# A bidirectional linear recurrence on one core: a table of steps for each compute engine in place of one common order

## What is computed

```python
def wkv_step(S, inp):                      # for each direction and each of 8 heads, S is 64 x 64
    r, w, k, v, a, b = inp
    sa = jnp.einsum('dbhvk,dbhk->dbhv', S, a)
    S = S * w[..., None, :] + sa[..., None] * b[..., None, :] + v[..., None] * k[..., None, :]
    return S, jnp.einsum('dbhvk,dbhk->dbhv', S, r)

S_c, y_c = wkv_bidir(S0, *prep_c[:6])      # context, both directions
_, y_l = wkv_bidir(S_c, *prep_l[:6])       # sequence, from the context's states
rwo_l = rwkv_output(y_l, prep_l, r_k, gn_w, gn_b)
g = jax.nn.sigmoid(gates)                  # gates = h @ w_in[:, ...], 3 x 1024 columns
merged = sum(g[n] * (branches[n] @ w_br[n]) for n in range(3))
```

## Time and profile before

| | us |
|---|---|
| median of three runs | 1972.29 |
| the three runs | 1978.79, 1972.29, 1966.57 |
| span of the profiled execution | 1977.8 |
| TensorE busy in it | 1749.3 (88%) |
| VectorE, ScalarE, POOL busy | 801.0, 518.5, 109.0 |
| mean granted TensorE clock | 0.939 of full speed |

### The profile page before, as it was taken

How to read it: one execution, slowest core, us unless ns; L and a number is a source line. 1 busy time by engine, 2 the same in 40 slices (tenths; PEclk the granted TensorE clock), 3 DMA queues, 4 the chain that set the end, 5 groups by cost and what they waited for, 6 DMA issues and landing times.

```text
span 1977.8 us, 37817 instructions
## 1 busy us (share of the span) xinstructions
PE 1749.3 (88%) x16766; PEld 936.9 (47%) x16766; DVE 801.0 (40%) x1472; ACT 518.5 (26%) x983; POOL 109.0 (6%) x143
## 2 busy tenths in 40 slices
PE   4999999989989999878988999899988987778786
PEld 3444565444546556345555666554543332323332
DVE  3753252646627464345444454325452211122111
ACT  3710252311127322344433431113131110000000
POOL 0000011010000000200000000000000101010100
PEclk8999997989989999989988997899988999998998
DMA  9121475252110200312221221236659999999996
GB/s 392 56 85 43 179 266 205 93 219 97 43 43 1 96 27 0 139 55 62 62 61 50 62 67 35 93 148 235 253 202 356 420 418 420 424 417 422 415 407 201
DMA packets 51560, 359.43 MB, mean 182 GB/s; under 512 B 8392, under 2 KB 8640, under 8 KB 32960
## 3 DMA queue, kind: packets, MB, share of 16 engines
q1 hardware_dynamic: 38896, 311.51, 39.5%
q0 software_dynamic: 12496, 45.45, 7.0%
HBM read 337.99 MB, written 27.32 MB: 185 GB/s over the span
## 4 chain that ended last, share of the span: by engine, by line
PE 69%; DMA 17%; DVE 6%; ACT 5%; issue 2%; POOL 0%; SPq 0%; DVEq 0%; ACTq 0%; POOLq 0%
PE psum L208 66%; DMA arena<-in_w 16%; ACT arena L205 4%; PE psum L211 3%; DVE arena L155 3%; ACT L205 1%; DVE arena L185 1%; DVE arena L165 1%; DVE arena L161 1%; DMA arena<-in_norm_post 1%; DVE arena L193 0%; DMA arena<-in_subln 0%; DVE arena L160 0%; DVE arena L181 0%; DVE arena L173 0%
## 5 line engine op out<-in xcount | busy, mean ns | idle before, releaser
L208 PE MATMUL psum<-arena 32*32 32x16 f32 (+11 forms) x16114 | 1668.5, 309 | 200.0 <-DMA arena<-in_w 82.5
L208 PEld LDWEIGHTS psum<-arena 32*32 32x32 f32 (+5 forms) x16114 | 863.6, 137 | 949.7 <-issue 784.8
L205 ACT ACTIVATE arena<-psum 128x512 f32<-128x512 f32 (+5 forms) x334 | 171.1, 512 | 920.8 <-PE psum L208 714.7
L155 DVE TENSOR_TENSOR arena<-arena,psum 128x512 f32<-128x512 f32 (+3 forms) x128 | 64.9, 507 | 427.7 <-PE psum L208 236.3
L155 DVE TENSOR_TENSOR arena<-arena 128x512 f32<-128x512 f32 (+10 forms) x315 | 191.6, 608 | 47.5 <-DMA arena<-in_norm_post 12.4
L205 ACT ACTIVATE arena<-psum,arena 128x128 f32<-128x128 f32 (+3 forms) x221 | 111.5, 505 | 305.8 <-PE psum L211 154.2
L205 ACT ACTIVATE arena<-arena 128x512 f32<-128x512 f32 (+10 forms) x254 | 138.8, 546 | 195.4 <-DVE arena L155 38.4
L155 DVE TENSOR_TENSOR arena<-psum,arena 128x128 f32<-128x128 f32 (+3 forms) x116 | 47.4, 409 | 194.3 <-PE psum L208 170.5
L211 PE MATMUL psum<-arena 128*128 128x128 f32 x652 | 101.4, 291 | 18.3 <-DMA arena<-fd,arena 8.9
L165 DVE SCALAR_TENSOR_TENSOR arena<-arena 128x512 f32<-128x512 f32 (+7 forms) x158 | 102.1, 646 | 38.2 <-ACT arena L205 33.1
L211 PEld LDWEIGHTS psum<-arena 128*128 128x128 f32 x652 | 75.4, 146 | 80.1 <-issue 52.9
(11 more groups left out here) (49 smaller groups left out, 176.7 us busy)
## 6 DMA issues: line engine op xcount, KB each, us to landing
arena<-in_w SPq DMA_DIRECT2D x127, 2048.0 KB, 25.6
arena<-in_w SPq DMA_DIRECT2D x48, 256.0 KB, 3.0
arena<-in_w SPq DMA_DIRECT2D x10, 1024.0 KB, 26.8
arena<-kd POOLq DMA_DIRECT2D x28, 256.0 KB, 3.8
gd<-arena SPq DMA_DIRECT2D x24, 256.0 KB, 3.2
arena<-gd SPq DMA_DIRECT2D x24, 256.0 KB, 8.4
arena<-in_w POOLq DMA_DIRECT2D x2, 2048.0 KB, 10.0
kd<-arena POOLq DMA_DIRECT2D x2, 1536.0 KB, 9.2
```

What stands on the lines that cost most here:

```text
L155: return self.ends(self.e.tensor_tensor(out, a, b, op))
L205: return self.ends(self.e.activation(out, a, func, **kw))
L208: return self.ends(self.e.matmul(out, lhs, rhs, start=start, stop=stop))
```

## The change

The common order is gone, and with it `WOVEN`, `rec_order` and `gate_steps`. Three tables, written out as text, give each compute engine its own list: `TENSOR_STEPS` (395 entries, 93 of them `gate`), `VECTOR_STEPS` (230) and `SCALAR_STEPS` (130, 24 of them `gate`). `gate` stands for two gate products on TensorE and for the copy of one block on ScalarE. As before, 6 gate products come ahead of the recurrence. Both directions now start together.

Four steps are divided where they wait inside: `kn` into `kn0`, `kn1` and `co` on TensorE; `a` into `gv` and `a` on TensorE; ScalarE's `p1` into `w` and `p1` (one group of four sigmoids each); VectorE's `p2` into `ls` (the scan) and `p2`. The finish's steps `f` have fewer empty places. What each step issues is the same, and each engine has as many instructions as before. POOL gets one more wait.

```diff
-FIRST_GATES = 6
-def gate_steps(order):
...
+FIRST_GATES = 3
+TENSOR_STEPS = """
+p1.00 p1.10 gate gate gate gate gate g1.00 gate g2.00 gate gate gate g1.10 gv.000 x1.00 a.000 kn0.00 g2.10 gate gate gv.100 u1.00 a.100 x1.10 kn0.10
...
+s.151 a.051 gate s.051 m.151 y.15 end.1 m.051 gate y.05 end.0 gate gate gate
+"""
+VECTOR_STEPS = """
+a.000 ls.00 a.100 p2.00 p3.00 ls.10 g1.00 p2.10 p3.10 g2.00 g1.10 x1.00 g2.10 u1.00 x1.10 u1.10 x2.00 x2.10 ls.01 u2.00 x3.00 p2.01 u3.00 p3.01 x4.00
...
+SCALAR_STEPS = """
+w.00 p1.00 gate p2.00 w.10 p1.10 gate p2.10 gate a.000 kn.00 kn.10 w.01 gate p1.01 p2.01 w.11 p1.11 gate a.100 p2.11 gate s.000 a.001 kn.01 s.001 w.02
...
+def steps(text):
+    for s in text.split():
+        name, at = (s.split(".") + [""])[:2]
+        yield (name, *map(int, at), *[0] * (3 - len(at)))
...
@@ gate_tensor
-                    yield
+                    if k % 2:
+                        yield
@@ rec_tensor
-            elif step == "kn":
-                for j in range(2):
-                    T.wait_ge(*ps.take(ring, "kn", d, n, j))
...
+            elif step in ("kn0", "kn1"):
+                j = int(step[2])
+                T.wait_ge(V["kb%d" % j, d, n], *ps.take(ring, "kn", d, n, j))
...
+            elif step == "co":
                 if lat(d, n):
...
-            elif step == "a":
+            elif step == "gv":
                 p = B.halves[h_]
                 T.wait_ge(V["g", d, n, "k"], *ps.take(B.bank, "x0", d, n, h_))
...
                 T.then_inc("gv", d, n, h_)
+            elif step == "a":
+                p, b = B.halves[h_], ps["x0", d, n, h_]
                 T.wait_ge(T["gv", d, n, h_], V["mp", d, 2 * n + h_])
@@ rec_scalar
-            if step == "p1":
-                for k, (dst, b0) in enumerate(((B.sig, "w0"), (B.ag, "a0"))):
+            if step in ("w", "p1"):
+                k, dst, b0 = (0, B.sig, "w0") if step == "w" else (1, B.ag, "a0")
@@ rec_vector
-            if step == "p2":
+            if step == "ls":
...
                 V.scan(L[:, back], MM["rs%d" % d][:, back], sig[:, back]).then_inc("ls", d, n)
+            elif step == "p2":
                 V.wait_ge(A["wa", d, n, 1], A["e2a", d, n])
@@ merge_gpsimd
-            G.wait_ge(T["lu", 0, 5, 5], V["tu", 0, 5])
+            G.wait_ge(T["lu", 0, 5, 5], T["co", 0, 5], V["tu", 0, 5])
@@ tensor_program
-            for i, step in enumerate(ORDER):
-                rec_tensor(*step, fin)
-                for _ in range(GATE_STEPS[i]):
+            for step in steps(TENSOR_STEPS):
+                if step[0] == "gate":
                     next(gates)
+                else:
+                    rec_tensor(*step, fin)
```

More of the change, by code:

```diff
@@ L26 @@
 NCOL = 53100
-WOVEN = 14
 SMALL = 1902
@@ L323 @@
 MAIN_CHUNKS = [0, 1, 2, 3, 6, 7, 8, 9, 10, 11, 4, 5, *range(14, 24), 12, 13, 24, 25, *range(26, 34), *range(40, 45)]
-FIRST_GATES = 6
-def gate_steps(order):
-    busy = [i for i, s in enumerate(order) if s[0] not in ("f", "end")]
-    share = [0] * len(order)
-    for i in busy:
-        share[i] = 2 if i < WOVEN or i > busy[-1] - 2 * WOVEN else 1
-    total, out, done = sum(share), [], 0
-    for i in range(len(order)):
-        n = 2 * round((96 - FIRST_GATES // 2) * sum(share[:i + 1]) / total)
-        out.append(n - done)
-        done = n
-    return out
+FIRST_GATES = 3
@@ L1720, in build, with finish_tensor @@
         last_read = lambda: (V["kb0", 0, 5], V["e2", 0, 5], V["kb0", 1, 5], V["e2", 1, 5])
-        def finish_tensor(c, ring, wait):
+        def finish_tensor(c, ring, n):
             i = c - 2
-            for _ in range(4):
+            for _ in range(4 * (n == 5)):
                 yield
@@ L1728, in finish_tensor @@
             T.mm(ps["fg", c], SG[:, c4(i)], G2, True, True).then_inc("fg", c)
-            for _ in range(1 + wait):
+            for _ in range(1 + 5 * (n == 5)):
                 yield
@@ L1735, in finish_tensor, with finish_scalar @@
             yield
-        def finish_scalar(c, st, wait):
-            yield
+        def finish_scalar(c, st, n):
+            for _ in range(n == 5):
+                yield
             A.wait_ge(V["fv", c])
             A.act(st[:, 16:24], st[:, 8:16], ACT.Sqrt, bias=eps[:, 1:2], scale=1.0 / 64).then_inc("fr", c)
-            for _ in range(4 + wait):
+            for _ in range(1 + 8 * (n == 5)):
                 yield
@@ L2782, in vector_program @@
             V.wait_ge(*end4())
-            for step in ORDER:
+            for step in steps(VECTOR_STEPS):
                 rec_vector(*step, fin)
@@ L2803, in scalar_program @@
             proj3_scalar()
-            fin = {}
             A.wait_ge(*end4())
-            for i, step in enumerate(ORDER):
-                rec_scalar(*step, fin)
-                for j in GATE_END.get(i, ()):
-                    gate_scalar(j)
+            fin = {(d, n): finish_scalar(recs[d].order[n], recs[d].stg, n) for d in range(2) for n in (4, 5)}
+            done_gates = iter(range(24))
+            for step in steps(SCALAR_STEPS):
+                if step[0] == "gate":
+                    gate_scalar(next(done_gates))
+                else:
+                    rec_scalar(*step, fin)
             merge_scalar([fin[0, 5], fin[1, 5]])
```

90 lines of the change are left out of this document (43 added, 47 removed).

## The result

The changed kernel takes 1920.83 us (median of four runs, 1913.70 to 1923.38) against 1971.48 for the kernel before in the same comparison: a ratio of 0.9715 with an interval of 0.9654 to 0.9776. The two medians alone would give 0.9743, which lies in that interval. A second comparison (after_2) gave 0.9687 (0.9647 to 0.9726). So the gain is 56 to 62 us by these ratios and 51 by the first comparison's medians. Some executions of either kernel take 2 to 3% longer at a lower granted clock, and the ratios leave them out. The two traces shown belong to runs of 1978.79 and 1913.70 us, the slowest of before and the fastest of now; their spans, 1977.8 and 1911.8 us, lie 66 us apart.

What follows compares the result with a forecast made beforehand. TensorE's amount of work was taken to bound the recurrence. Idle time -29 (-14.4 - 19.2 + 5) and clock -17 gave -46 on the profiled span of 1977.8, 1932; less 5.5 for the median, 1926 us, range 1903 to 1957.

Steps and rivals of the forecast that it cites:

- the stage: Recurrence from the first p1 to the last gate pair: to last about 459 us instead of 505.
- Head, -14.4: Start of the recurrence, 806 to 862 us: gate pairs and both p1 fill TensorE's waits; 18.4 us idle falls to 4.
- Body, -19.2: Recurrence, 862 to 1276 us: six TensorE pauses before g2 (13.3 us) and two others go, as p2 is cut.
- New waits, +5: Recurrence: thinner cover of the state chain and long steps in other queues add two pauses; bounds 0 and 21 us.
- The thin cover of `a` and `s`: State chain on TensorE: only 1.8 us of steps between a and s, in 7 of 24 pairs; enough if ScalarE is free.
- Clock, -17: Recurrence: 92 us at half clock cost 30 us; 51/92 of that comes back as long pauses go.
- The clock fell without pauses: Recurrence: half-clock stretches such as at 978 had no long pause ahead, so not all 30 us would come back.
- The pause beside the merge's first weights: Near the recurrence's end: one TensorE pause of about 3 us stays but moves, as the merge's weights load beside gate weights.
- The pauses before g2 stay: Rival: two PSUM banks a direction are too few in any order; 1946 us, up to 1962; 14%.
- Little happens: Rival: thin cover of the state chain eats the head's gain through new short pauses; 1955 to 1980 us; 8%.
- The gate bank: Rival, slower: gate products wait for ScalarE's copies out of their one bank, 4.9 us behind one p2; 1995 us; 4%.
- Everything comes back: Rival: short pauses go too, idle from 61.7 to 20 us, and the clock's 30 us with them; 1900 us; 13%.

Runs made afterwards that it cites:

- after_2: The changed kernel unaltered, run for a second trace and timing; ratio 0.9687 to the kernel before.
- p2_up: Changed kernel with each p2 in VectorE's table moved up directly behind its ls; ratio 0.9805 to the kernel before.
- p2_split_alone: Kernel before, common order kept, with only VectorE's p2 cut, its rest three slots after the scan; ratio 0.9942 to the kernel before.
- p2_joined: Changed kernel with each ls in VectorE's table put back directly ahead of its p2, where p2 stands; ratio 0.9929 to the kernel before.
- gates_by_step: Kernel before, common order and undivided steps, with gate pairs behind the steps where the changed kernel has them; ratio 1.0166 to the kernel before.

## Why the prediction was right, and where not

The direction, the stage and the one-to-one passage to the end held, and the time lies in the range (1926 forecast, 1921 measured). That the two are so close is in part luck. Forecast was a gain of 46 us; the ratios say 56 and 62, and it is the first comparison's medians, 51 us apart, that come nearest. The stage lost 67 us in the mean of the two pairs of traces; about 5 of them are lost again ahead of the stage, whose start differs from run to run (804 to 811 us before, 810 to 815 after). Of the signs named, the stage (459 us forecast, 435 and 438 measured) and its idle time (33; 24.1 and 21.5) missed on the same side; the clock over the stage, 0.96 and 0.95, lay in its range. Step by step:

- **Head, -14.4.** From 18.4 to 5.4 us (49.00 less 43.60): -13.0. The forecast 4 us of pauses were 4.7, at the places named, though the one behind g1 was 2.45 where 1.1 stood in the sum. Right.
- **Body, -19.2.** All six pauses before g2 and both others went. Pauses ended by an engine fell from 50.4 to 6.4 us in the whole stage, so the many short ones, which I let stay, went too. The term was under-sized. The mechanism holds (p2_up, p2_split_alone), but it was half of it: the wait in p2 has two sides, and I priced only VectorE's, worth 23 us (p2_up). Where ScalarE waits for the scan as well, the price is 45 (p2_joined); 25.5 us of that second wait stood in the kernel before.
- **New waits, +5.** By an engine 1.7 us in two, 1.02 and 0.69, both at a gate pair behind a copy. The thin cover of `a` and `s` was enough each time. "Issue" rose from 9.1 to 17.9 us instead, which I had not priced. The idle sum, -29, was -36.6 (-38.4 in the second pair).
- **Clock, -17.** I took 30 us for what 92 us at half clock cost, the middle between 15 and 46. The traces of the table but gates_by_step agree on one relation: stage less idle less half of the half-clock time is 389 to 399 us, and a straight line through the 13 makes it 0.49 us for a microsecond at half clock. So a microsecond at half clock costs about half a microsecond, the upper bound: 48 before. (gates_by_step, with 153.6 us, is at 384, which with it makes the slope 0.43.) Of it 22 to 32 came back. This term was mis-sized most, by 10 us in the mean, and in its basis: a slope of a half means that nearly all of the stage's work, and not the gate products alone, takes twice as long at half clock.
- **The clock fell without pauses.** This was wrong. Ahead of the stretch at 978 stood a pause of 1.55 us ended by "issue" (TensorE at 977.36), which I had passed over, looking only at the long ones:

```profile
977.36 12.35 PE L208 MATMUL psum<-arena 32*32 32x16 f32 x265 [1.55 <-issue]
```

  The sum with all of the 30 us was 13 us larger than mine; in direction the table bears it out (more idle time, mostly more half-clock time), but 31 to 58 us at half clock remain with 21 to 27 us of idle time. The Trainium skill's rule ("TensorE: Matmul & The Clock Gate", HAM oscillation) on idle gaps stood behind that sum; this case's traces agree in the direction, and show stretches at half clock with no gap of 3 us.
- **The pause beside the merge's first weights** did not come. In the kernel before it was a wait for instructions (above); whether those loads had held up the packet is not shown.

The rivals. *The pauses before g2 stay*, with what the Trainium skill says of buffers ("Perfetto Trace Analysis", Identifying Performance Opportunities) as a possible cause: refuted in the common order itself, where they shrank by two thirds with the same banks. *Little happens*: no new pause stands at an `a` or an `s`. *The gate bank*: 5.4 us in these tables (1.25, 2.45, 1.02 and 0.69), but gates_by_step shows that it can be more, 7.2 us of ScalarE's time behind one misplaced copy. *Everything comes back* (1900) was nearest in mechanism: idle time of 21 to 24 us where it said 20; the clock kept a third to a half of its price.

What the prediction did not see is that the parts don't add up. The cut in p2 alone gains 11 us, bringing the directions together costs 14, the gate places alone cost 33; and in the changed kernel, p2's division taken back costs some 45, the gate places some 55. The sum by pauses came near because it read what the pauses wait for in the finished orders, not because each edit has a value. Which of the many short pauses a given placement closes stays open; it was not tried pair by pair, nor was direction 1's late start within the new tables.

## What to carry to other kernels

A step with a wait inside has to be placed on both engines: ask what stands behind the wait on the engine that waits, and what stands behind its producer on the other. Filler work is worth what its exact places are worth, and its completion (a copy out of the bank) needs a place of its own, behind the critical chain. Where TensorE bounds a stage, as here, price about half of every microsecond at half clock, and read the short pauses ahead of it. Before you put a pause without a releaser down to an engine or a load, look for a packet of the instruction queue that ends just ahead of its end.

## What the hardware showed that I had not expected

- Pauses of 0.5 to 2.6 us with no releaser, mostly in the middle of a run of tiny products: 16 in 435 us, 17.9 us in all, most of the idle time that is left. Those of 1 us and more end 1.2 to 1.6 us after a 16 KB packet of the instruction queue has ended. They sum to 11 to 24 us in the other kernels but one, and to 9.1 and 8.5 in the two traces of the kernel before.
- With idle time of 24 to 27 us, the time at half clock ranged from 30.7 to 58.0 us among kernels, and it differed by 10 us between two traces of one kernel (41.0 and 30.7 us): by the relation above, 5 us of scatter from run to run.
- A plain re-placement of filler products in an otherwise unchanged order cost 33 us (16 to 50).
